# Square sums of two tiles as two half-width matmuls side by side, and their roots spread by ScalarE, in the first key unit of a dilated-attention stage

## The reference, cut to what matters

```python
def rms_norm(t, w):
    t32 = t.astype(jnp.float32)
    return t32 * lax.rsqrt(jnp.mean(t32 * t32, axis=-1, keepdims=True) + NORM_EPS) * w.astype(jnp.float32)

proj = hn @ w_in                       # (2048, 1024) @ (1024, IN_WIDTH)
u_f, g_f, q, k, v, g_a = jnp.split(proj, SPLIT_POINTS, axis=-1)
q = rms_norm(q.reshape(B, S, N_ATTN_HEADS, HEAD_DIM), q_norm_w) * HEAD_DIM ** -0.5
k = rms_norm(k.reshape(B, S, N_ATTN_HEADS, HEAD_DIM), k_norm_w)
...
o_c, lse_c = dilated_window_attention(q[:, :, sl], k[:, :, sl], v[:, :, sl], window, dilation, slopes)
alpha = jax.nn.softmax(jnp.stack(lses, axis=0), axis=0)      # over the three dilations
o = jnp.sum(alpha[..., None] * jnp.stack(outs, axis=0), axis=0)
```

## Time and profile before

| what | value |
|---|---|
| median of 3 runs | 3391.24 us (3390.47 to 3391.63) |
| the profiled execution's own time | 3391.35 us |
| its span | 3389.6 us |
| mean granted TensorE clock | 0.992 |
| PE busy | 3300.9 us (97%) |
| DVE, ACT, POOL busy | 1298.0, 1018.5, 920.0 us (38%, 30%, 27%) |

### The profile page before, as it was taken

How to read it: one execution, slowest core, us unless ns; L and a number is a source line. 1 busy time by engine, 2 the same in 40 slices (tenths; PEclk the granted TensorE clock), 3 DMA queues, 4 the chain that set the end, 5 groups by cost and what they waited for, 6 DMA issues and landing times. The chain is left out here.

```text
span 3389.6 us, 43856 instructions
## 1 busy us (share of the span) xinstructions
PE 3300.9 (97%) x16379; PEld 1806.4 (53%) x16379; DVE 1298.0 (38%) x2804; ACT 1018.5 (30%) x2409; POOL 920.0 (27%) x705
## 2 busy tenths in 40 slices
PE   7999999998999999999999999999999999899999
PEld 3485858584455454444445544554455455445544
DVE  3343434346244243444224322342243324545522
ACT  4314141413234143233134422442343234311100
POOL 1002020204532533633321125113411341161232
PEclk9999999999999999999999999999999999999999
DMA  7101010103120212332111133113211321240321
GB/s 233 30 24 38 21 38 13 33 24 100 40 48 17 50 29 87 107 109 84 52 35 39 44 85 81 39 50 89 71 39 54 92 65 39 63 114 13 143 93 62
DMA packets 229949, 210.82 MB, mean 62 GB/s; under 512 B 69404, under 2 KB 194732, under 8 KB 225600
## 3 DMA queue, kind: packets, MB, share of 16 engines
q1 hardware_dynamic: 226636, 208.01, 21.0%
q10 hardware_dynamic: 3104, 0.01, 0.1%
HBM read 157.98 MB, written 50.01 MB: 61 GB/s over the span
## 5 line engine op out<-in xcount | busy, mean ns | idle before, releaser
L2461 PE MATMUL d<-hT,roll 128*128 128x512 f32 x1280 | 582.5, 599 | 2.1 <-PEq L76 2.1
L2461 PE MATMUL d<-w_room,roll 128*128 128x512 f32 x960 | 434.9, 596 | 0.0
L2461 PEld LDWEIGHTS d<-hT,roll 128*128 128x128 f32 x1280 | 239.7, 191 | 292.5 <-issue 290.6
L600 PE MATMUL m<-hT,roll 128*128 128x512 f32 x704 | 321.1, 593 | 1.3 <-ACT pre L750 1.3
L2461 PEld LDWEIGHTS d<-w_room,roll 128*128 128x128 f32 x960 | 178.9, 190 | 213.2 <-issue 210.0
L2498 POOL TENSOR_TENSOR w_z<-w_u,w_y 128x512 f32<-128x512 f32 x40 | 50.8, 1270 | 725.6 <-ACT w_y L2467 725.6
L1412 PE MATMUL n<-hT,roll 128*128 128x512 f32 x512 | 226.5, 597 | 1.8 <-PEq L76 1.8
L3158 ACT ACTIVATE mix_f<-sneg,negmax 128x192 f32<-128x192 f32 (+1 forms) x384 | 160.9, 420 | 108.4 <-DVE negmax L3310 107.8
L600 PEld LDWEIGHTS m<-hT,roll 128*128 128x128 f32 x704 | 124.9, 191 | 116.0 <-issue 115.8
L1412 PE MATMUL n<-mix_na,roll 128*128 128x512 f32 x384 | 169.4, 594 | 1.7 <-POOL roll L1312 1.7
L548 POOL TENSOR_TENSOR hn<-hn 128x512 f32<-128x512 f32 x16 | 17.5, 1092 | 544.3 <-DVE hn L917 544.3
(11 more groups left out here) (403 smaller groups left out, 5206.0 us busy)
## 6 DMA issues: line engine op xcount, KB each, us to landing
roll<-in_w_in SPq DMA_DIRECT2D x128, 256.0 KB, 3.1
mix_f<-alpha SPq DMA_DIRECT2D x48, 192.0 KB, 6.3
xg<-in_x SPq DMA_DIRECT2D x4, 2048.0 KB, 16.8
roll<-in_w_in SPq DMA_DIRECT2D x16, 512.0 KB, 3.8
rb<-r_rows SPq DMA_DIRECT2D x16, 512.0 KB, 4.9
mix_ml<-in_x SPq DMA_DIRECT2D x16, 512.0 KB, 3.4
x<-mix_ml SPq DMA_DIRECT2D x16, 512.0 KB, 3.0
o_rows<-mix_f SPq DMA_DIRECT2D x8, 1024.0 KB, 5.1
```

What stands on the lines that cost most here:

```text
L600: last = nc.tensor.matmul(bank[n % 2][:], w[:, k], hT[:, k, (n % 4) * TB:(n % 4 + 1) * TB], start=(k == 0), stop=(k == KC - 1))
L2461: last = nc.tensor.matmul(bank[self.bank_of(n, j, i)][:], w[:, k], x[k], start=(k == 0), stop=(k == h - 1))
```

## The change

Only the first key unit of each group and the start of the values unit behind it change (`cfg(a) == 1`). PE no longer sums each of the 8 tiles by a 128-column matmul. `pair_sums(a, r)` takes tiles 2r and 2r + 1 together: two matmuls whose weights are columns 32 to 95 of `ones` (32 columns for head 0, 32 for head 1), the first of which writes partitions 0 to 63 of `S_BANK` and the second partitions 64 to 127. ACT takes the logarithm of both in one instruction, in place in PSUM (`pair_log`, L3154), and then makes the roots of one tile by four exponentials of 32 partitions each (`spread_root`, L3161), which spread each head's 32 rows over its 64 partitions. The pairs stand behind products (0,7), (1,3), (1,7) and behind (0,3) of the values unit; the norms on DVE move back accordingly, the last three into the values unit. The queues of SP and GpSimd keep their order.

```diff
@@ PE
+def pair_sums(a, r):
+    if a == 0 and r == 0:
+        pe.wait_ge(consts, 64)
+    pe.wait_ge(squared, 8 * a + 2 * r + 2)
+    if r == 0:
+        need(pe, v_dve, 2 * a)
+    else:
+        pe.wait_ge(recip, 8 * a + 2 * r)
+    for e in range(2):
+        nc.tensor.matmul(bank[S_BANK][e * half:(e + 1) * half], ones[:, half // 2:half // 2 + half], sq[:, e], start=True, stop=True).then_inc(ssq, 1)
+
+def project_first_keys(a):
+    n = keys_of(a)
+    for j in range(2):
+        for i in range(1, 8):
+            project(n, j, i)
+            r = {(0, 7): 0, (1, 3): 1, (1, 7): 2}.get((j, i))
+            if r is not None:
+                pair_sums(a, r)
...
 def project_values(a):
-            if j == 0 and i == 1:
-                sums(a, 7)
+            if j == 0 and i == 3:
+                pair_sums(a, 3)
@@ ACT
+def pair_log(a, r):
+    act.wait_ge(ssq, 8 * a + 2 * r + 2)
+    nc.scalar.activation(bank[S_BANK][:], bank[S_BANK][:], ACT.Ln, bias=epst[:, 0:1], scale=1.0 / half).then_inc(rooted, 2)
+
+def spread_root(a, e):
+    act.wait_ge(rooted, 8 * a + e // 2 * 2 + 2)
+    need(act, ready, 8 * a + e - 1)
+    for i in range(4):
+        at, to = e % 2 * half + i // 2 * (half // 2), i * (half // 2)
+        last = nc.scalar.activation(rt[to:to + half // 2, e % 2], bank[S_BANK][at:at + half // 2], ACT.Exp, scale=-0.5)
+    last.then_inc(recip, 1)
+
+def project_first_keys(a):
+    n, g = keys_of(a), a // N_CFG
+    hold(n, 0, 1)
+    hold(n, 0, 4)
+    square(a, 0)
+    if g > 0:
+        late.factors_act(nc, act, g - 1)
+    square(a, 1)
+    pair_log(a, 0)
+    square(a, 2)
+    spread_root(a, 0)
+    hold(n, 1, 1)
+    spread_root(a, 1)
+    square(a, 3)
+    pair_log(a, 1)
+    square(a, 4)
+    spread_root(a, 2)
+    hold(n, 1, 4)
+    spread_root(a, 3)
+    square(a, 5)
+    pair_log(a, 2)
+    square(a, 6)
+    spread_root(a, 4)
...
 def project_values(a):
         hold(n, j, 1)
         if j == 0:
-            root(a, 7)
+            spread_root(a, 5)
+            square(a, 7)
+            pair_log(a, 3)
+            spread_root(a, 6)
         hold(n, j, 4)
+        if j == 0:
+            spread_root(a, 7)
@@ DVE, first keys: add(0,2) add(0,3) add(0,5) add(0,6) add(0,7) norm 0, add(1,2) norm 1, add(1,3) norm 2,
@@ add(1,5) norm 3, add(1,6) add(1,7) norm 4; values: add(0,2) norm 5, add(0,3) norm 6, add(0,5) norm 7
```

More of the change, by code:

```diff
@@ L3105, in _ @@
                         project_first_values(a)
-                    project_keys(a)
-                    if cfg(a) == 1:
+                        project_first_keys(a)
                         project_values(a)
+                    else:
+                        project_keys(a)
                 for slot in range(1, NB + 5):
@@ L3213, in project_first_values @@
                         attend(a - 1, slot)
+                def project_first_keys(a):
[21 more added lines that the diff above has]
+                    spread_root(a, 4)
                 def project_keys(a):
-                    n, g = keys_of(a), a // N_CFG
-                    b = a - 1 if cfg(a) != 1 else -1
+                    n = keys_of(a)
+                    b = a - 1
                     hold(n, 0, 1)
@@ L3222, in project_keys @@
                     square(a, 0)
-                    if g > 0 and cfg(a) == 1:
-                        late.factors_act(nc, act, g - 1)
                     for slot in (4, 5):
@@ L3377, in project_first_values, with project_first_keys @@
                             attend(a - 1, 7 * j + i)
+                def project_first_keys(a):
+                    n, g = keys_of(a), a // N_CFG
+                    add(n, 0, 2)
+                    add(n, 0, 3)
+                    if g > 0:
+                        late.lower_dve(nc, dve, g - 1)
+                    add(n, 0, 5)
+                    if g > 0:
+                        late.invert_dve(nc, dve, g - 1)
+                    add(n, 0, 6)
+                    add(n, 0, 7)
+                    norm(a, 0)
+                    add(n, 1, 2)
+                    norm(a, 1)
+                    add(n, 1, 3)
+                    norm(a, 2)
+                    add(n, 1, 5)
+                    norm(a, 3)
+                    add(n, 1, 6)
+                    add(n, 1, 7)
+                    norm(a, 4)
                 def project_keys(a):
-                    n, g = keys_of(a), a // N_CFG
-                    b = a - 1 if cfg(a) != 1 else -1
-                    weighing = g > 0 and cfg(a) == 1
+                    n = keys_of(a)
+                    b = a - 1
                     attend(b, 1)
@@ L3387, in project_keys @@
                     attend(b, 3)
-                    if weighing:
-                        late.lower_dve(nc, dve, g - 1)
                     attend(b, 4)
@@ L3392, in project_keys @@
                     attend(b, 5)
-                    if weighing:
-                        late.invert_dve(nc, dve, g - 1)
                     for i in (6, 7):
@@ L3417, in project_values @@
                     n = keys_of(a) + 1
-                    norm(a, 7)
                     for j in range(2):
@@ L3422, in project_values @@
                         if j == 0:
+                            norm(a, 5)
                             need(dve, pv, NB * a)
@@ L3425, in project_values @@
                         add(n, j, 3, cols(0))
+                        if j == 0:
+                            norm(a, 6)
                         add(n, j, 5)
+                        if j == 0:
+                            norm(a, 7)
                         add(n, j, 6)
```

5 lines of the change are left out of this document (2 added, 3 removed).

## The result

The changed kernel takes 3400.88 us (median of 7 runs, 3398.81 to 3403.23) against 3391.24 us before (7 runs, 3389.85 to 3393.14). The ratio is 1.0029, with a 95% interval of 1.0019 to 1.0038: slower, by 9.6 us. That is only 0.3%, but the whole interval lies above 1. The forecast was 3396.2 with a range up to 3400, so the result lies 0.9 us outside it. The profiled execution of the changed kernel took 3400.63 us (span 3398.8), that of before 3391.35 (span 3389.6). Among the experiments' runs, one of e3 (3501.14 us, mean granted clock 0.945) and one of e6 (5885.7 us, 0.606) were in a slower state, and the ratios leave them out.

A forecast was written before the change was run, and what follows sets the result against it. PE, busy 97% of the span, was taken to bound the kernel. From 3391.35 us, -2.2 (group 1), +2.1 (later weights) and +5.1 (clock) gave 3396.3, stated as a 3396.2 median; range 3388 to 3400.

The forecast's parts named there:

- A pair costs 1.16 us: On PE, two half-width sums overlap, 0.86 us plus 0.30 for changing shape, instead of 1.72; saves 0.56, lower bound 0.49.
- Group 1 gives 2.2 us, the longer chains hold: Group 1 has no combining; four pairs save 0.56 us each, and the longer logarithm, root and norm chains delay nothing.
- The three waits for ACT go: In groups 2 to 4, PE's 1.8 us waits for tile 5's square vanish, as it is wanted 3.43 us later.
- PE waits 4.4, 4.9 and 4.4 us at product (0,2) for L2410: Values unit, groups 2 to 4: PE arrives early and waits for GpSimd's weights; with group 1's gain, nearly no net change.
- The chain behind L2410 moves by 0.3 us ahead: Groups 2 to 4: combine(2), block 3's load and the weights come 0.3 us sooner, bounds 0 and 1.1.
- The clock falls to 0.50 and costs 1.7 us a wait: Behind the three waits at product (0,2), PE runs at half clock; 5.1 us lost in all, bounds 0 and 7.7.
- the first (2.6 us or more a wait, 3399): Rival: the wait moves to product (0,2) and the clock falls for longer, +7.7 us in all; chance 0.15.
- That the clock holds: Rival: the wait moves to product (0,2) but PE's clock does not fall, -0.1 us, 3391.1; chance 0.12.
- That the wait goes for good: Rival: block 3 comes 4.4 us sooner, so all pairs and waits count, 14.3 us won, 3377; chance 0.12.
- That the pairs don't overlap: Rival: at 512 columns a pair's matmuls run one after the other, 2.02 us each; +5.9 us, 3397; chance 0.06.

The follow-up runs named there:

- e3: Changed kernel with four unread 128-column matmuls between products (0,1) and (0,2) of the values unit in groups 2 to 4; 3392.05 us.
- e6: Kernel before, without pairs, with block 3's load ahead of the transfers waiting for combine(2) and join(n,1,2) ahead of combine(2); 3386.12 us.
- e1: Changed kernel with raw block 3's load issued ahead of the fetch and store that wait for combine(2) in SP's queue; 3378.78 us.
- e5: Changed kernel with block 3's load ahead of the transfers waiting for combine(2), and join(n,1,2) ahead of combine(2) on GpSimd; 3377.64 us.
- e4: Changed kernel with the norms of tiles 0 and 1 in groups 2 to 4's first key units cut to 4 columns per residue; 3394.67 us.
- e7: Changed kernel with block 3's load moved ahead and both matmuls of a pair writing the same 64 partitions, one after the other; 3391.01 us.

## Why the prediction was wrong

The course was the one forecast: the pairs save time, the wait moves to product (0,2), and the clock falls behind it. But one step, the chain behind L2410, went the other way, and one term, the clock, was too small. Taken step by step:

- *A pair costs 1.16 us.* It costs 1.21. The 0.05 that I took off the 0.37 for changing shape, as the wait of a short first pass, is there after all: in group 1's first pair the second pass starts 0.48 us behind the first, not 0.43. The lower bound, 0.49 saved, was nearly the truth (0.51).
- *Group 1 gives 2.2 us, the longer chains hold.* 2.04 us, 0.2 less by the four dearer pairs, and PE waits nowhere. A 32x512 exponential out of PSUM takes 0.587 us, and I had taken 0.585 from the 128x512 copy of the earlier trace rows. ScalarE's groups with shapes kept apart:

```profile
L3161 ACT ACTIVATE rt<-d 32x512 f32<-32x512 f32 x128 | 75.2, 587 | 1.6
...
L3154 ACT ACTIVATE d<-d,eps 128x512 f32<-128x512 f32 x16 | 10.6, 662 | 75.7 <-PE d L2984 75.7
```

- *The three waits for ACT go.* In the main they did, 1.8 us each, but three others came at pair 2: 0.90, 1.15 and 0.57 us. One part is that join 2 got later, by 0.9 us in group 2. The other is a slip of mine: the square is wanted not 3.43 us later but 14 x 3.43 + 2 x 1.16 - (13 x 3.43 + 5 x 0.86) = 1.4 us later, as PE has less to do ahead of it, and that is less than the 1.8 us of delay of before. It cost nothing here, as it only shortened the wait at (0,2). It becomes visible once that wait is gone (e1), and e5 takes it away by moving the join.
- *PE waits 4.4, 4.9 and 4.4 us at product (0,2) for L2410.* Right in place and releaser, and near in size: 4.23, 4.56 and 4.11. Two errors cancel here. PE came later, held up by pair 2, and so did the weights.
- *The chain behind L2410 moves by 0.3 us ahead.* **This step failed.** It moved back by 0.7, 0.8 and 0.2 us. I had taken from the earlier trace rows that the piece for `combine(2)` lands at U + 43.0 and kept that time as fixed. But the fetch waits for `combine(0)`, and I had worked out myself that norm 0 runs from about U + 28.6 to 29.7. `combine(0)` starts at U + 28.9. I never laid the two beside each other. The bounds of 0 and 1.1 us ahead didn't hold a move back. e4 shows the cause. The sizes differ by 1.0, 1.1 and 0.5 us: 2.6 together.
- *The clock falls to 0.50 and costs 1.7 us a wait.* It fell, and each wait cost 2.4, 2.4 and 2.9: 7.7 against 5.1. **This term was sized too small.** Of the two rows I took the one with 1.7, by the likeness of the work around it. But that likeness is not what decides. In the row with 1.7 PE was at work again at 1423.05 and in that trace the clock is at 1.00 until 1424.1, so PE worked only 3.4 us at 0.50. Behind the other gap, and behind all three waits here, it was at 0.50 from PE's first matmul on. The row with 2.6 lost was the better guide, and 7.7 was the bound that I had named.

The errors add up: 0.2 in group 1, 2.6 for the chain, 2.6 for the clock and 3 x 0.05 for the pair behind each wait are 5.5 us, from the +5.0 forecast to the +10.5 of the stretches. The rest of the program gave back 1.3 us in the profiled executions, and the median was 4.7 us above the forecast. The range had room for the clock at its bound (3399), but not for that together with a chain that moved back.

As to the rivals: the first (2.6 us or more a wait, 3399) was nearest, 1.9 us under the median, and it too lacked the chain's 2.6. That the clock holds was wrong in the changed kernel. It came true in e3, where PE had been kept at work. That the wait goes for good is what e1 and e5 make happen, at 3378.8 and 3377.6 against the 3377 worked out. That the pairs don't overlap is refuted by e7.

What stays open: at what moment of a wait the clock falls and how long it stays at 0.50. The traces show that these two set the loss (1.7 to 2.95 us in the six waits of the changed kernel and e4), and that the length of the wait doesn't; what sets them is not shown. And it was not tried whether moving the norms on VectorE clear of `combine(0)` would do as well as moving the load.

## What to carry to other kernels

- When a wait is removed and another input was only 0.4 us early, the change is worth nothing until that input is moved too. Here one line in SP's queue, a load put ahead of transfers that wait for somebody else, turned 9.6 us lost into 12.6 won.
- A wait of 3 to 5 us on a PE that runs dense matmuls costs more than its length, by 1.7 to 3 us here: half of the time that PE then works at a granted clock of 0.50. Price it from the profile's own windows behind such gaps, look in them at when the clock fell, and take the dearer row.
- When a step is moved in time, look at what runs on VectorE and GpSimd at its new place, and follow the slower one to the DMA that waits for it.

## What the runs showed of the hardware

- A norm on VectorE (128x512, two SBUF inputs) and an addition on GpSimd don't run side by side. The addition that started second took 2.05 us instead of 1.27 and 1.47 instead of 0.73, and both were back with the norms cut to a few columns (e4). A norm that started second took 2.11 instead of 1.14.
- Behind a wait of 3.0 to 4.9 us PE's granted clock was 0.50, and product (0,2) lost half of the time that PE worked at it: 3.4 us in one of six waits, 4.8 to 6.0 in the others. Behind waits of 1.2 and 1.5 us it stayed at 1.00 (e3, and the earlier trace rows).
- Two matmuls with 64 columns of weights, 512 columns of data and outputs on different halves of the partitions overlap entirely: their four records took 1.08 us, and 1.93 when both wrote the same half. Going to this shape and back cost 0.35 us each time (1.21 - 0.86).
- The same load took 6.4 to 6.9 us to land behind the coefficients of a piece, and 2.7 to 3.1 us ahead of them (changed kernel and e1, groups 2 to 4).
